# Moving the arena of activations to a multiple of 256 bytes in a two-block transformer kernel

## The reference

```python
def first_block(...):
    h = concatenate([meta, x])                                   # 272 tokens x 2048
    h = h + hybrid_mixer(rmsnorm(h, norm_mix), w_in, ..., w_out)
    h = h + swiglu(rmsnorm(h, norm_ffn), w_gate, w_up, w_down)   # 2 x (2048 x 5632), 5632 x 2048
    return rmsnorm(h, final_norm)[:, 16:]

def second_block(x, c, ctx, c_ctx, w_mod, ...):
    sh1, sc1, gt1, sh2, sc2, gt2 = split(silu(c) @ w_mod + b_mod, 6)
    h = rmsnorm(x, g_attn) * (1 + sc1) + sh1
    x = x + gt1 * (concatenate([o_mla, o_na, o_fn]) @ w_out)
    h2 = rmsnorm(x, g_ffn) * (1 + sc2) + sh2
    x = x + gt2 * conv_ffn(h2, w_up, conv_w, conv_b, w_down)
    return rmsnorm(x, g_final)
```

## The kernel before

| buffer | first byte before | mod 256 | first byte after | mod 256 |
|---|---|---|---|---|
| raw, hi, lo (16384 bytes each) | 16512, 32896, 49280 | 128 | same | 128 |
| tabs | 101888 | 0 | same | 0 |
| mp | 111360 | 0 | 111360 | 0 |
| gm | 111424 | 64 | same | 64 |
| pick | 111616 | 0 | 111392 (mp's slot + 32) | 32 |
| att | 111680 | 64 | 111616 | 0 |
| std, rstd | 111936, 113984 | 64 | 111872, 113920 | 0 |
| work_slab | 116032 | 64 | 115968 | 0 |
| arena | 124736 | 64 | 124672 | 0 |

## Time and profile before

### The profile page before, as it was taken

The page is one execution under the profiler, slowest core; times in us unless marked ns, Lnnn a source line. Parts: engine busy times, 40 slices in busy tenths (PEclk is TensorE's granted clock), DMA queues, the critical chain, the costliest instruction groups (busy, mean ns, idle before and its releaser), DMA issues.

```text
span 2352.1 us, 49789 instructions
## 1 busy us (share of the span) xinstructions
PE 2342.0 (100%) x19292; PEld 2279.5 (97%) x19292; DVE 1663.2 (71%) x2501; ACT 1123.4 (48%) x1500; POOL 0.2 (0%) x4
## 2 busy tenths in 40 slices
PE   9999999999999999999999999999999999999998
PEld 9998899999999999999988989799999999999998
DVE  6676678788877878888887755456666566655675
ACT  6354445544445554445632332455555355544554
POOL 0000000000000000000000000000000000000000
PEclk9999999999999999999999999999999999999999
DMA  7875566588778887787657722054565665666664
GB/s 284 285 272 195 188 233 233 198 285 303 273 255 283 280 285 240 264 290 270 224 200 258 258 80 93 22 175 166 192 196 194 194 191 187 199 193 191 197 192 143
DMA packets 141889, 509.19 MB, mean 216 GB/s; under 512 B 15824, under 2 KB 17360, under 8 KB 141392
## 3 DMA queue, kind: packets, MB, share of 16 engines
q1 hardware_dynamic: 141776, 507.60, 64.1%
HBM read 505.44 MB, written 2.10 MB: 216 GB/s over the span
## 4 chain that ended last, share of the span: by engine, by line
PE 99%; DVE 0%; DMA 0%; ACT 0%; SPq 0%; issue 0%; ACTq 0%
PE ps L1175 30%; PE ps L1177 30%; PE ps L1176 30%; PE ps L1517 1%; PE ps L1203 1%; PE ps L1205 1%; PE ps L1204 1%; PE ps L1535 1%; PE ps L1349 1%; PE ps L1526 0%; PE ps L1330 0%; PE ps L1374 0%; PE ps L1583 0%; PE ps L1355 0%; DMA raw<-in_stream 0%; PE ps L1331 0%
## 5 line engine op out<-in xcount | busy, mean ns | idle before, releaser
L1717 DVE TENSOR_TENSOR lo<-raw,hi 128x1024 fp32r<-128x1024 f32 x753 | 918.4, 1222 | 489.4 <-ACT hi L584 485.1
L584 ACT ACTIVATE hi<-raw 128x1024 fp32r<-128x1024 f32 x753 | 797.0, 1061 | 969.3 <-PE ps L1177 864.0
L1175 PE MATMUL ps<-hs,hi 128*128 128x256 f32 (+1 forms) x3056 | 860.7, 282 | 0.4 <-DVE hs L2526 0.3
L1176 PE MATMUL ps<-hs,hi 128*128 128x256 f32 (+1 forms) x3056 | 859.8, 281 | 0.0
L1177 PE MATMUL ps<-hs,lo 128*128 128x256 f32 (+1 forms) x3056 | 859.8, 281 | 0.0
L1176 PEld LDWEIGHTS ps<-hs,hi 128*128 128x128 f32 x3056 | 576.2, 189 | 5.0
L1175 PEld LDWEIGHTS ps<-hs,hi 128*128 128x128 f32 x3056 | 573.7, 188 | 6.2 <-DVE hs L2526 0.8
L1177 PEld LDWEIGHTS ps<-hs,lo 128*128 128x128 f32 x3056 | 573.7, 188 | 5.1
L1175 PE MATMUL ps<-hid,hi 128*128 128x256 f32 x1408 | 388.7, 276 | 0.0
L1176 PE MATMUL ps<-hid,hi 128*128 128x256 f32 x1408 | 388.6, 276 | 0.0
L1177 PE MATMUL ps<-hid,lo 128*128 128x256 f32 x1408 | 388.6, 276 | 0.0
(11 more groups left out here) (323 smaller groups left out, 2537.2 us busy)
## 6 DMA issues: line engine op xcount, KB each, us to landing
raw<-in_stream SPq DMA_DIRECT2D x753, 512.0 KB, 4.3
wm<-in_mod_stream SPq DMA_DIRECT2D x192, 512.0 KB, 4.8
out_tokens<-y_final SPq DMA_DIRECT2D x4, 512.0 KB, 3.7
h<-in_tokens SPq DMA_DIRECT2D x3, 544.0 KB, 8.7
cx<-in_ctx_tokens SPq DMA_DIRECT2D x6, 256.0 KB, 6.0
cbx<-in_c_rows SPq DMA_DIRECT2D x1, 1024.0 KB, 8.0
cbc<-in_c_rows SPq DMA_DIRECT2D x1, 1024.0 KB, 5.5
na<-in_na_bias SPq DMA_DIRECT2D x1, 1024.0 KB, 4.8
```

The source lines that it names most:

```text
L584: act.activation(hi[:, slot, :], raw[:, slot, :], ACT.Copy).then_inc(hi_done, 1)
L1175: pe.matmul(acc_, hi[:, slot, w], x_hi, start=kt == 0, stop=False)
L1176: pe.matmul(acc_, hi[:, slot, w], x_lo, start=False, stop=False)
L1717: dve.tensor_tensor(lo[:, slot, :], raw[:, slot, :], hi[:, slot, :].bitcast(F32), ALU.subtract)\
```

## The change

It gives `mp` and `pick` one slot of 64 bytes, which moves everything between `gm` and the arena down by 64 bytes, and it rounds the arena's start up to a multiple of 256. The rounding adds nothing, since the new start is 487 x 256. No instruction is added, removed or reordered; only addresses differ.

```diff
-        mp, _ = keep("mp", [P, 3, 2])
+        _, o_mp = keep("mp_pick", [P, 16])
+        mp = at("mp", [P, 3, 2], F32, o_mp)
+        pick = at("pick", [P, HEADS], F32R, o_mp + 32)
         gm, _ = keep("gm", [P, 3, KT])
-        pick, _ = keep("pick", [P, HEADS], F32R)
         att, _ = keep("att", [P, 3, 2 * HEADS])
         cq, _ = keep("cq", [P, 2, HEADS])
@@
-        arena = top[0]
+        arena = -(-top[0] // 256) * 256
```

## The result

The changed kernel takes 2423.86 us (median of 4 runs, 2421.73 to 2424.89), where the kernel before takes 2351.35 us beside it: 72 us slower. The ratio is 1.0265, with a 95% interval of 1.0201 to 1.0330.

A forecast was written before the change was run, and what follows sets the result against it. TensorE, busy throughout at full clock, was taken to bound the kernel by its matmul pace. All parts of the change summed to 0, so the forecast was the old median, 2350 us, with a range of 2300 to 2400.

The forecast's parts named there:

- the parts put at nothing: mp and pick sharing a slot, and std, rstd, work_slab and vector reads moving 64 bytes: each forecast at cost 0.
- the price of a nanosecond: About 15,700 fixed-remainder 256-wide matmuls on TensorE, so 1 ns in each is 15.7 us.
- part 4: TensorE's arena operands, from remainder 64 to 0 against weights at 128: the only lever, forecast at unchanged paces, sum 0.
- the trace's own trial: by_token, with hi and lo at remainder 128 against activations at 64, shows the same 113.3 ns as the other layout.
- The step before it: up1b and up1c share code and addresses but differ by 4.5 ns a matmul, so address alone does not set the pace.
- 11.1 ns of surplus in kv1: kv1's 272-wide matmuls with changing remainders: 126.8 ns against an estimated 115.7; on 256 columns, an upper bound of 120 ns.
- The bound below: Floor for 256-column matmuls, 109 ns, from plain float32 times halved; 4.3 ns under the fast pace, 8.8 under the slow.
- Slower: Rival: remainder 0 against weights at 128 collides more in main matmuls, up to +91 us, 2441 us; chance 0.14.
- Another deal of the paces: Rival: the shift changes which layers take 113.3 or 117.8 ns, 2336 to 2406 us; chance 0.25.
- Aligned rows reach the floor: Rival: moving rows touch four 256-byte blocks instead of five, saving up to 82 us, 2268 us; towards the floor, chance 0.19.
- The argument against it from the 512-wide rows: In joint, 17.6 ns surplus for ten blocks and 4.3 ns for five do not scale, so blocks do not set it.
- The seams read from the earlier trace: Four one-column matmuls before up1b precede the slow pace, four 128-column ones before dn1b the fast; a phase was guessed.

The follow-up runs named there:

- slot_only: Changed kernel with the arena's start moved up 64 bytes, back to remainder 64, the shared slot kept: 10 runs, 2351 to 2384 us, ratio 1.0052.
- program of its own: Separate programs, no kernel changed, that only load, round and multiply in stretches with set remainders for rows and weights: 113.3 to 120.0 ns a matmul at 256 columns.
- arena128: Kernel before with the arena 64 bytes higher, at remainder 128, weights at 128, so distance 0: 2440.80 us, ratio 1.0358.
- ring64: Changed kernel with gm placed ahead of hi, so weights at remainder 64, arena at 0: five runs at 2352 to 2354 us, five at 2379 to 2382, ratio 1.0047.
- arena192: Kernel before with the arena 128 bytes higher, at remainder 192, weights at 128, so distance 64: 2403.45 us, ratio 1.0140.

## Why the prediction was wrong

The forecast was 2350 us with a range of 2300 to 2400; the kernel came out at 2423.86. What bounds the kernel was read rightly: TensorE's pace and nothing else. So were the parts put at nothing, the slot and the moved vector buffers, which slot_only bears out, and the price of a nanosecond (15.7 us for each): 12,500 matmuls at 5.3 ns and 3,200 at 1 to 2 give the 70 us.

The step that failed is part 4, where the cost of the new addresses was put at 0 because by_token was called the trace's own trial of another layout. It has the moving rows at 128 and the stationary operand at 64, which was taken as a second address that gave the same pace, and so as a sign that addresses do not count. The experiments show what it is: distance 64, the mirror of 192, and of the four distances at steps of 64 those two have the same two numbers, 113.3 and 117.8. The trial was of the one kind of move that leaves the set as it is. The change went to distance 128, which no row of before had with a fixed remainder, and which costs 118.7 or 120.0.

The step before it failed too. That up1b and up1c differ at the same addresses shows that the address does not decide alone; it was then used as if the address decided nothing. In the runs the distance gives the set of paces, and something else chooses in it.

The only rows that met distances 0 and 128 were those of xs1, which walk through all four remainders, with 11.1 ns of surplus in kv1. They could not have settled it. The program of its own has 123.3 to 126.7 ns at 272 columns for single distances, 7.6 to 11.0 ns over the same estimate, and distance 64 is as dear there as 128. So the 11.1 needs hardly any mixing, but it speaks of the width of 272 as much as of the distance.

The bound below, 109 ns, was worked out from 430 ns at 512 columns, which is one of the two records of a plain float32 matmul and not the whole of it. Half of that record was a guess, and no stretch came down to it.

The rivals, one by one:

- *Slower* was the right one, and was given 0.14. It said that remainder 0 against weights at 128 is a new pair and priced 6.7 ns on the fast matmuls as the bound, 2441 us. The changed kernel's pair costs 5.3 ns (118.7); distance 0 costs the full 6.7, and arena128 came out at 2440.80 us, on the bound. That it lies on the bound is in part luck, since the 120 ns were carried over from 272 columns, where distance 0 itself costs 125.3 and not 126.8. What was wrong is the chance, and with it the range.
- *Another deal of the paces* was not what the change did, but it is real: slot_only, ring64 and the kernel before have runs 28 us apart, as priced, in slot_only by the second feed-forward's pace, and arena192 had the slow one nearly everywhere (2403.45 against 2406). The kernel before had shown it ahead of the prediction, with 2382.15 among its three executions; the prediction took the median and did not ask what that run was.
- *Aligned rows reach the floor*: no stretch went under 113.3 ns. The argument against it from the 512-wide rows held up for a reason that was not the one given, since their pace hangs on the distance too. The Trainium skill (TensorE: Matmul & The Clock Gate, "Back-to-back issue gap") has N / 2.4 + 2.5 for an isolated matmul, 109.2 ns here; these float32r matmuls, each with its own weights, measured 113.3 to 120.0.

The seams read from the earlier trace rows as one-column to slow and 128-column to fast were too neat: the programs of their own show either pace after the same seam. That a pace once taken is kept to the end of a stretch is borne out; that the seam by itself sets it is not shown.

The tests named at the end of the prediction worked: "a third number appears in all fixed-remainder layers, near 109 or above 118, in hs and hid alike", with the 512-wide layers and conv1 nearly unmoved and kv1 1.2 ns quicker, a little over the nanosecond allowed.

## What to carry to other kernels

Where TensorE is busy throughout, divide a stretch by its number of matmuls: two paces for one shape at one clock are a lever, here 4% of the whole kernel between its dearest layout and its best (2440.80 and 2341.64 us). When a pace may hang on addresses, look at the distance between the two operands, not at the roundness of one; a multiple of 256 for both is among the dearest of the layouts measured here at 256 columns (120.0 ns), and the best distance depends on the width. Before a row of the trace is taken as a trial of the new layout, ask whether it differs from the old one in the quantity that matters, or is its mirror.

## What the hardware showed beyond that

- The pace of float32r matmuls of 256 columns took only about a dozen values, from 113.3 to 120.0 ns, and in the kernels a layer kept its value over hundreds of matmuls. Distances of 320 and 448 bytes had the numbers of 64 and 192, as a period of 256 has it. The Trainium skill (SBUF — State Buffer, "SBUF: two separate sides") says that TensorE never waits on anyone, in a passage on contention between engines, and no run here tests that. TensorE's own two streams, the moving rows and the weights, do not run free of one another in these runs, at up to 6.7 ns in 113.3.
- In the program of its own, 128-column matmuls with rows and weights at distance 128 came every 111.7 ns. In the next stretch of the same width, with TensorE busy throughout, the granted clock fell to half, the 1.2 GHz level, and 128 columns took 213.3 ns. It was back at 2.4 GHz in the stretch of 272 columns. The stretches before, in and after:

```profile
426.00:437.00 11.00, 11.00 (x101) 1.00 0.01 1
437.00:458.00 21.00, 21.00 (x114) 0.57 0.00 1
460.00:500.00 40.00, 40.00 (x190) 0.50 0.00 0
518.00:530.00 12.00, 12.00 (x100) 1.00 0.01 1
```
